# When VectorE normalises attention probabilities, and when it takes two of four remainders

## The reference

```python
s = jnp.einsum('bhnqd,bhrnkd->bhnqrk', q_r, k_r) * scale
bias = jnp.transpose(rpb_cols[:, ridx], (0, 2, 3, 1, 4))
s = jnp.where(mask, s + bias, -jnp.inf)
p = jax.nn.softmax(s, axis=(-2, -1))
return jnp.einsum('bhnqrk,bhrnkd->bhnqd', p, v_r)
```

## Time and profile before

| | us |
|---|---|
| median of 3 runs | 1368.54 |
| lowest and highest run | 1366.41 and 1369.21 |
| profiled execution, its own time | 1367.6 |
| span of that execution | 1365.8 |
| TensorE busy in the span | 1302.9 (95%) |
| VectorE busy | 910.1 (67%) |
| ScalarE busy | 582.7 (43%) |
| GpSimd busy | 488.6 (36%) |
| TensorE's granted clock, mean of the execution | 0.989 |

### The profile page before, as it was taken

How to read it: one execution, slowest core, us unless ns; L and a number is a source line. 1 busy time by engine, 2 the same in 40 slices (tenths; PEclk the granted TensorE clock), 3 DMA queues, 4 the chain that set the end, 5 groups by cost and what they waited for, 6 DMA issues and landing times.

```text
span 1365.8 us, 18052 instructions
## 1 busy us (share of the span) xinstructions
PE 1302.9 (95%) x6624; PEld 1094.8 (80%) x6624; DVE 910.1 (67%) x1250; ACT 582.7 (43%) x1034; POOL 488.6 (36%) x260
## 2 busy tenths in 40 slices
PE   5998999999999999989998999999999999999998
PEld 4976777898888888878786778888888788888887
DVE  5455677641597786975756655555554888888885
ACT  6235656544443443333144544554454343233341
POOL 5232211123322132211613444444443455445452
PEclk9999999999999999999999999999999999999999
DMA  8341332222110111023420264444548844353433
GB/s 240 123 115 31 72 91 78 74 68 75 45 31 16 32 32 31 16 93 139 124 87 22 91 197 162 137 147 154 162 136 305 298 154 156 104 206 122 139 94 137
DMA packets 138533, 154.93 MB, mean 113 GB/s; under 512 B 11472, under 2 KB 97744, under 8 KB 138448
## 3 DMA queue, kind: packets, MB, share of 16 engines
q1 hardware_dynamic: 132976, 147.04, 33.6%
q10 hardware_dynamic: 5472, 6.75, 1.5%
HBM read 109.72 MB, written 44.04 MB: 113 GB/s over the span
## 4 chain that ended last, share of the span: by engine, by line
PE 84%; DVE 9%; issue 3%; ACT 3%; DMA 1%; POOL 0%; ACTq 0%; DVEq 0%
PE bank L2165 8%; PE bank L2169 7%; PE bank L2168 7%; PE bank L2134 7%; PE bank L2137 7%; PE bank L2138 7%; PE bank L1882 5%; PE bank L1886 5%; PE bank L1885 5%; PE bank L1966 4%; PE bank L2093 2%; PE bank L2097 2%; PE bank L2096 2%; PE bank L1869 2%; PE bank L1873 2%
## 5 line engine op out<-in xcount | busy, mean ns | idle before, releaser
L813 POOL TENSOR_TENSOR w_hi<-stage,one_col 128x1024 fp32r<-128x1024 f32 x36 | 71.5, 1986 | 460.6 <-PE bank L1882 346.0
L868 POOL TENSOR_TENSOR a_split<-a_raw,a_split 128x1024 fp32r<-128x1024 f32 x56 | 148.1, 2661 | 166.5 <-ACT a_split L1136 166.5
L2134 PE MATMUL bank<-set,w_hi 128*128 128x512 f32 x448 | 180.1, 402 | 5.5 <-DVE s L1705 2.6
L2137 PE MATMUL bank<-set,w_hi 128*128 128x512 f32 x448 | 177.8, 397 | 0.0
L2138 PE MATMUL bank<-set,w_lo 128*128 128x512 f32 x448 | 177.6, 397 | 0.0
L2165 PE MATMUL bank<-w_hi,a_split 128*128 128x512 f32 x448 | 174.6, 390 | 0.2
L2169 PE MATMUL bank<-w_hi,a_split 128*128 128x512 f32 x448 | 174.3, 389 | 0.0
L2168 PE MATMUL bank<-w_lo,a_split 128*128 128x512 f32 x448 | 174.3, 389 | 0.0
L1882 PE MATMUL bank<-uT_hi,w_hi 128*128 128x512 f32 x384 | 160.8, 419 | 6.5 <-DVE h_gate L1370 6.4
L1886 PE MATMUL bank<-uT_hi,w_lo 128*128 128x512 f32 x384 | 151.6, 395 | 0.0
L1885 PE MATMUL bank<-uT_lo,w_hi 128*128 128x512 f32 x384 | 151.0, 393 | 0.0
(11 more groups left out here) (208 smaller groups left out, 2832.7 us busy)
## 6 DMA issues: line engine op xcount, KB each, us to landing
a_raw<-a_dram SPq DMA_DIRECT2D x56, 512.0 KB, 3.7
a_dram<-abuf SPq DMA_DIRECT2D x111, 256.0 KB, 2.1
stage<-in_w_in SPq DMA_DIRECT2D x32, 512.0 KB, 4.2
raw<-in_w_down SPq DMA_DIRECT2D x10, 1024.0 KB, 8.1
stage<-in_w_up SPq DMA_DIRECT2D x16, 512.0 KB, 5.3
raw_b<-in_w_up SPq DMA_DIRECT2D x16, 512.0 KB, 5.5
x_tok<-in_x SPq DMA_DIRECT2D x8, 512.0 KB, 5.4
v_dram<-vs ACTq DMA_DIRECT2D x32, 128.0 KB, 1.8
```

The lines of the kernel that those rows point to most:

```text
L868: pool.tensor_tensor(split_of(m, 1), a_raw[:, m % 4, :, :], split_of(m, 0).bitcast(F32), ALU.subtract).then_inc(b_lo, 1)
L2134: first = pe.matmul(dst, w[0], u[0], start=k == 0 and p in (1, 5, 6, 7), stop=False, skip_group_check=True)
L2137: pe.matmul(dst, w[0], u[1], start=False, stop=False, skip_group_check=True)
```

## The change

Only the order on VectorE in the attention loop is changed. The first half of the normalisation of a step (groups 0 and 1) stood at the end of the turn in which the step was masked; it now stands in the next turn, behind the first two remainders and ahead of the second half. The third remainder stands ahead of the root product, the fourth between root product and bias; both stood behind the bias.

```diff
                 if s - 1 >= -2 and s + 1 < STEPS:
+                    normalise_probs(s + 1, 0)
                     normalise_probs(s + 1, 2)
                 if -2 <= s - 1 <= 9:
                     qk_lo(BEFORE + s - 1)
+                if 0 <= s < STEPS:
+                    take_pT(s, 2)
                 if qk is not None:
                     qk_product(qk)
+                if 0 <= s < STEPS:
+                    take_pT(s, 3)
                 if s + 2 < STEPS:
                     build_bias(s + 2)
-                if 0 <= s < STEPS:
-                    take_pT(s, 2)
-                    take_pT(s, 3)
-                if s + 2 < STEPS:
                     for g in range(NG):
                         mask_scores(s + 2, g)
-                    normalise_probs(s + 2, 0)
```

## The result

| | before | with the change |
|---|---|---|
| median of the runs, us | 1368.62 (6 runs) | 1374.68 (6 runs) |
| lowest and highest run | 1366.41 and 1371.03 | 1371.20 and 1376.24 |
| span of the profiled execution | 1365.8 | 1371.2 |

The ratio is 1.0038, with a 95% interval of 1.0023 to 1.0054: slower by 3 to 7 us. I had forecast 2.4 us and a range that ended at 1373.5, so the median lies 1.2 us above it.

The account below looks back on a forecast made before the run. TensorE, busy 95% of the span, bounds the kernel; VectorE's first mask sets the odd steps' pace. Terms 2.86 + 0.70 + 0.28 - 1.42 = +2.4 us gave a median of 1371.0, range 1367.0 to 1373.5.

Parts of the forecast that it names:

- odd steps: Steps 3, 5, 7: first mask later by 0.77 us each; step 1: 0.55; together +2.86. Step 9, without GpSimd: +0.70.
- third score tiles: Keys-queries products needing the same step's first mask instruction over; in odd steps forecast to start 0.15 us behind that mask.
- the first and third products: TensorE's matmuls with the values needing first and third remainder; step 5's 0.56 us gain at the first forecast lost again.
- step 13's: First product no longer late behind a pair GpSimd held; the one gain that stays, -1.42 us.
- even steps: Steps 2, 4, 6, 8: added VectorE run mostly meets slack; 0.15, 0, 0.13 and 0 us, together +0.28.
- steps 10 and 13: Step 10: slack at the third score tile, nothing reaches TensorE, 0. Step 13: first product's wait goes, -1.42 us.
- The waits on VectorE's own result: Product no longer waiting for the key remainder saves 0.19 us; mask now waiting for the bias just written costs 0.11.
- The moved pairs: Normalisation TENSOR_SCALARs behind the first two remainders; in step 5 forecast held to GpSimd's second instruction's end, 197.37 us.
- slip: Faster rival: in steps 1, 3, 5, 7 moved TENSOR_SCALARs get the port before GpSimd's second instruction; -4.9 us, 1363.7; chance 0.08.
- the wait of turn -1: Steps -2 and -1 keep their order, so they were forecast at 0.

Follow-up runs that it names:

- the filled kernels: Changed kernel plus unread matmuls ahead of the third score tile in turns 1, 3, 5, 7, 9: six, 1371.44 and 1371.89 us; three, 1371.16 us.
- the filled wait in turn -1: Kernel before, with 14 additional unread matmuls inside TensorE's 4.05 us wait in turn -1: 1366.44 us, ratio 0.9983.
- the kernel with only turn 13 changed: Kernel before, with the first half of the normalisation moved into the next turn for turn 13 alone: 1366.20 us without one outlier, ratio 0.9982.
- between the masks up to turn 8: Normalisation halves between masks in turns -1 to 8, turn 10's at the end of turn 8, then the change's order; against before: 1359.53 us, ratio 0.9932.
- half the change: Kernel before with only the first normalisation half moved into the next turn, third and fourth remainder left behind the bias: 1375.88 us, ratio 1.0050.
- the normalisation between the masks: Both normalisation halves of step s + 1 behind masks 1 and 2 of step s + 2, remainders as in the change; against before: 1368.87 us, ratio 1.0005.

## Why the prediction was wrong

**The direction and the mechanism of the waits were right.** The odd steps' third score tiles follow the mask, the gains at the first and third products are lost there, and step 13's stays. By step, in us, from the starts of TensorE's matmuls without the stretches at the lower clock:

| step | 1 | 2 | 3 | 4 | 5 | 6 | 7 | 8 | 9 | 10 | 13 | sum |
|---|---|---|---|---|---|---|---|---|---|---|---|---|
| forecast | 0.55 | 0.15 | 0.77 | 0 | 0.77 | 0.13 | 0.77 | 0 | 0.70 | 0 | -1.42 | 2.4 |
| measured | 0.50 | 0.24 | 0.84 | 0.12 | 0.73 | 0.23 | 0.83 | 0.11 | 0.70 | -0.11 | -1.68 | 2.5 |

That the sums agree to 0.1 is partly luck: the even steps cost 0.4 us more than forecast, and steps 10 and 13 gave 0.4 back that I hadn't counted.

The waits on VectorE's own result were rightly priced: 0.60 behind the key remainder where the product had started after 0.79. I had called the Trainium skill ("VectorE: DVE Perf Modes", section "The DRAIN you can't avoid") contradicted by this. It isn't, quite: its statement that the semaphore costs nothing extra is of eight copies in a row, and the section says too that a next instruction which isn't held starts earlier. The trace agrees with the latter, by 0.19 and 0.11 us. The moved pairs were held to the end of GpSimd's second instruction; the "slip" didn't occur in any profile. (Its first mask, "at about 200.2", would be 196.74 + 3.32 = 200.06 by the prediction's own distances; nothing else hangs on it.)

**The step that failed** is the one from TensorE's waits to the time. I counted a wait at its length. I had written that what is won at the first and third products is "lost again" at the third score tile, as if two waits of 0.56 and 1.17 us were the same as one of 0.74 and one of 1.89 close behind it. They are not: behind waits of 1.7 to 1.9 us at the third score tile the granted clock fell in two of five turns in either profile, and each stretch cost 1.3 to 1.6 us. The clock stood nowhere in the sum, at nothing and without a reason. Two such stretches, 3.0 us, were missing; with them 2.4 becomes 5.4 (measured from turn 1 on: 5.36 and 5.35), and the ratios 1.0038 and 1.0043 are 5.2 and 5.9 us. No rival had this either, so the range ended too low. The row that would have told it is not among those I read: the clock of 0.50 behind the wait of turn -1, a turn that I had set at 0 because its order stays.

What is shown, and what isn't: that the excess comes from the clock is shown by the filled kernels (no fall in turns 1 to 9 in any profile, the stage at +2.4 and not +5.4, the runs 2 to 3 us faster than the change) and by the filled wait in turn -1. Why the clock falls behind one such wait and not behind the next isn't settled by these runs. Nor is the kernel before free of it: with its order in turns 1 to 9, the kernel with only turn 13 changed lost 1.1 us behind the third product of turn 9 (clock 0.51 from 246.90 to 250.40), while the profile of before did not. The change makes such stretches more frequent, by the mean clocks of the runs by about two in each; in which turns they fall is seen in the two profiles alone.

## What to carry to other kernels

A wait that goes from one place of TensorE to another is not gone; ask for each engine which instruction the bounding engine needs next, and count everything that stands ahead of it, from the last point where the feeding engine was idle. Work that has slack belongs where its engine waits anyway (here between the masks up to turn 8, to which some 4.7 of the 6.4 us of that profile's stage belong), and what that place has in turns of another kind must be looked at turn by turn. Where waits of TensorE merge or grow, look at the granted clock behind the waits that are already there, and price the stretch behind the new one.

## What the runs showed of the hardware

- TensorE's clock fell to its lower level behind waits of 0.74 and 1.89 us close together (0.53 granted over the next 3.6 us), behind single ones of 2.62 and 1.53 us (in the kernels with half the change and with the normalisation between the masks), in some turns and executions and not in others with the same waits; and six matmuls without a use, or three, in the wait kept it up. Filling a wait made the changed kernel 2 to 3 us faster.
- GpSimd's splitting of weights holds TENSOR_SCALAR (2.45 us for a pair of 0.68), and VectorE's TENSOR_TENSOR with both operands in SBUF as well: 5.55 us for four of 1.77 together, 2.77 for one of 0.68. TENSOR_TENSOR with one operand in PSUM (`pT_lo`) was not held beside it (0.88 us for two in step 5 of the kernel before, with and without GpSimd at work). The Trainium skill says so in "SBUF — State Buffer", section "Who interferes with whom", and the traces agree.
- Which of the two is held goes, in the rows of the kernel before, by who starts first, with some lead. At the end of step 0 a TENSOR_SCALAR started 0.07 us ahead of GpSimd's instruction, took its usual 0.42 us, and GpSimd's took 2.10 and not 1.90. At the end of steps 2 and 4 it started 0.01 us ahead and took 2.12 us.
- The first score tile started at 111.89 us in the kernel before and between 111.3 and 115.8 in the others, ahead of anything that had been changed. A comparison of two spans has this scatter in it; the comparison of a stage doesn't.
